# The front of the two expert stages, reordered: router ahead of the turns, inner scores behind the matrix of places, second exponential behind the gather

## The reference

```python
def hier_moe(h, router_g, router_g_b, router_e, router_e_b, w_gate, w_up, w_down):
    ...
    g_logits = (xt @ router_g + router_g_b).astype(f32)
    g_prob = jax.nn.softmax(g_logits, axis=-1)
    _, g_top = lax.top_k(g_logits, 1)
    p_group = jnp.take_along_axis(g_prob, g_top, axis=-1)
    e_logits = (jnp.einsum('td,gde->tge', xt, router_e) + router_e_b).astype(f32)
    e_sel = jnp.take_along_axis(e_logits, g_top[:, :, None], axis=1)[:, 0]
    top_v, top_i = lax.top_k(e_sel, TOP_K_INNER)
    top_w = jax.nn.softmax(top_v, axis=-1) * p_group
    inner = jnp.sum(jax.nn.one_hot(top_i, EXPERTS_PER_GROUP, dtype=f32) * top_w[..., None], axis=1)
    gates = jax.nn.one_hot(g_top[:, 0], N_EXPERT_GROUPS, dtype=f32)[:, :, None] * inner[:, None, :]
    out = jnp.zeros((xt.shape[0], d), f32)
    for gi in range(N_EXPERT_GROUPS):
        hid = jax.nn.silu(jnp.einsum('td,edf->tef', xt, w_gate[gi])) * jnp.einsum('td,edf->tef', xt, w_up[gi])
        hid = hid * gates[:, gi, :, None].astype(hid.dtype)
        out = out + jnp.einsum('tef,efd->td', hid, w_down[gi]).astype(f32)
    return out.reshape(bsz, s, d).astype(h.dtype)
```

## Time and profile before

| what | us |
|---|---|
| time, median of 3 runs (lowest to highest) | 3173.31 (3170.94 to 3181.55) |
| the profiled execution's own time | 3173.19 |
| its span in the trace | 3171.4 |
| busy: PE, DVE, ACT, POOL | 2880.9, 2026.5, 1645.3, 134.6 |
| chain that ended last, share of the span: PE, DVE, ACT, issue, DMA | 79%, 14%, 3%, 2%, 2% |

### The profile page before, as it was taken

The page is one execution under the profiler, slowest core; times in us unless marked ns, Lnnn a source line. Parts: engine busy times, 40 slices in busy tenths (PEclk is TensorE's granted clock), DMA queues, the critical chain, the costliest instruction groups (busy, mean ns, idle before and its releaser), DMA issues.

```text
span 3171.4 us, 54600 instructions
## 1 busy us (share of the span) xinstructions
PE 2880.9 (91%) x22896; PEld 2598.8 (82%) x22896; DVE 2026.5 (64%) x2543; ACT 1645.3 (52%) x2326; POOL 134.6 (4%) x164
## 2 busy tenths in 40 slices
PE   3778888689999999979999899999899979999999
PEld 3767666678877999867778788999799969998899
DVE  6866665579998555569999645444544684446444
ACT  1333342268887344448888535444544734445444
POOL 0013221000000020200000000000000000000000
PEclk7879999699999999979999989999899989999999
DMA  8630000259998537329999521554255404544253
GB/s 353 248 124 3 3 2 2 103 210 360 354 354 313 202 144 269 117 100 354 356 352 355 194 80 67 186 182 164 80 181 178 158 27 147 185 160 146 104 178 130
DMA packets 78119, 572.86 MB, mean 181 GB/s; under 512 B 8658, under 2 KB 8658, under 8 KB 9042
## 3 DMA queue, kind: packets, MB, share of 16 engines
q1 hardware_dynamic: 76752, 558.93, 47.3%
q10 hardware_dynamic: 1154, 10.90, 0.9%
HBM read 568.74 MB, written 1.05 MB: 180 GB/s over the span
## 4 chain that ended last, share of the span: by engine, by line
PE 79%; DVE 14%; ACT 3%; issue 2%; DMA 2%; DVEq 0%; POOL 0%; ACTq 0%; PEldq 0%
PE ps L1247 13%; PE ps L1174 12%; PE ps L811 9%; PE ps L812 9%; PE ps L813 9%; PE ps L1268 6%; DVE arena L2000 5%; DVE arena L1994 2%; DVE wl L1994 2%; DVE hl L1994 2%; DMA ring<-in_stream 1%; PE ps L832 1%; PE ps L831 1%; PE ps L830 1%; PE ps L853 1%
## 5 line engine op out<-in xcount | busy, mean ns | idle before, releaser
L1994 DVE TENSOR_TENSOR wl<-ring,wh 128x1024 fp32r<-128x1024 f32 (+1 forms) x560 | 937.8, 1695 | 636.1 <-ACT wh L1458 630.2
L1458 ACT ACTIVATE wh<-ring 128x1024 fp32r<-128x1024 f32 (+1 forms) x560 | 788.8, 1431 | 488.1 <-PE ps L813 323.0
L811 PE MATMUL ps<-hh,wh 128*128 128x256 f32 x2528 | 738.7, 292 | 79.5 <-DVE hl L1994 72.7
L812 PE MATMUL ps<-hh,wl 128*128 128x256 f32 x2528 | 725.8, 287 | 0.0
L813 PE MATMUL ps<-hl,wh 128*128 128x256 f32 x2528 | 725.2, 287 | 0.0
L811 PEld LDWEIGHTS ps<-hh,wh 128*128 128x128 f32 x2528 | 495.8, 196 | 94.3 <-issue 65.1
L812 PEld LDWEIGHTS ps<-hh,wl 128*128 128x128 f32 x2528 | 496.4, 196 | 3.2 <-issue 2.9
L813 PEld LDWEIGHTS ps<-hl,wh 128*128 128x128 f32 x2528 | 496.0, 196 | 0.0
L1174 PE MATMUL ps<-hidh,wh 128*128 128x256 f32 x1024 | 289.8, 283 | 0.0
L1174 PE MATMUL ps<-hidh,wl 128*128 128x256 f32 x1024 | 289.8, 283 | 0.0
L1174 PE MATMUL ps<-hidl,wh 128*128 128x256 f32 x1024 | 289.8, 283 | 0.0
(11 more groups left out here) (243 smaller groups left out, 4566.3 us busy)
## 6 DMA issues: line engine op xcount, KB each, us to landing
ring<-in_stream SPq DMA_DIRECT2D x532, 1024.0 KB, 5.0
arena<-in_wcmp ACTq DMA_DIRECT2D x2, 2048.0 KB, 11.2
arena<-in_lora ACTq DMA_DIRECT2D x1, 2048.0 KB, 10.9
arena<-in_atm ACTq DMA_DIRECT2D x1, 1762.0 KB, 8.3
x<-in_xT ACTq DMA_DIRECT2D x1, 1024.0 KB
out<-x SPq DMA_DIRECT2D x1, 1024.0 KB, 3.9
arena<-in_rwm ACTq DMA_DIRECT2D x1, 736.0 KB, 14.8
cols<-in_cols ACTq DMA_DIRECT2D x1, 719.0 KB
```

What stands on the lines that cost most here:

```text
L811: mm(out, w[0], h[0], start=first, stop=False)
L812: mm(out, w[1], h[0], start=False, stop=False)
L1458: return nc.scalar.activation(out, in_, ACT.Copy)
L1994: return v.tensor_tensor(out, a, b, op)
```

## The change

It changes the order of instructions in the front of both expert stages, and their banks and waits accordingly; the arithmetic is the same but for the order in which router products are summed.

- Router: one product writes the bias for both halves (72 columns), then the products of each pair of chunks follow as soon as the pair is there. The turns come behind the router, in the hi banks instead of the lo banks.
- VectorE: `norm` no longer does `flipped_low`; pair 0's low part comes behind the choice of the group, those of pairs 1 to 3 behind the eight blocks of the matrix of places. `m_P` counts after these eight blocks; the fifth part's two blocks have a count of their own, `m_P5`. `prep(q0 + 1)` moves from the start of the stage to behind the gather's low parts, and so do the inner scores.
- TensorE: the gather waits for the low part of each pair of chunks instead of all; `cleared` comes ahead of the wait for the gather's banks; `m_P5` is waited for ahead of the gather of the fifth part.
- ScalarE: the second exponential moves from behind the first casts of expert 1 to behind the gather's casts.

```diff
--- before.py
+++ after.py
@@ -333,8 +333,8 @@
 
 def _plan_moe(i):
     _plan(f"norm_cm{i}", 1)
-    _plan(f"xt{i}", 4)
     _plan(f"route{i}", 1)
+    _plan(f"xt{i}", 0, 4)
     _plan(f"rank{i}", 1)
     _plan(f"gather{i}", 8)
     _plan(f"moe{i}", 0, 4)
@@ -1196,20 +1196,23 @@
 
             def experts(i):
                 name, y0 = f"moe{i}", (AUX + 10) * i
+                t = claim("lo", LO[f"route{i}"])
+                route = [t[:, tt * 36:tt * 36 + 36] for tt in range(2)]
+                mm(t[:, 0:72].rearrange("p (t n) -> p t n", t=2), ones[0:1, :], rows[0:1, None, 36 * i:36 * i + 36].to_broadcast([1, 2, 36]),
+                   start=True, stop=False, skip_group_check=True)
                 for pr in range(4):
                     pe.wait_ge(src_ready, 4 * VER[name] + pr + 1)
-                    t = claim("lo", LO[f"xt{i}"] + pr)
+                    for k in (2 * pr, 2 * pr + 1):
+                        for tt in range(2):
+                            last = mm(route[tt], hf[:, k, tt * P:(tt + 1) * P], col(f"router{i}", 36 * k, 36), start=False, stop=k == C - 1,
+                                      skip_group_check=True)
+                last.then_inc(tile_ready["lo"], 1)
+                for pr in range(4):
+                    t = claim("hi", HI[f"xt{i}"] + pr)
                     for tt in range(2):
                         for k in range(2):
                             last = nc.tensor.transpose(t[:, (2 * tt + k) * P:(2 * tt + k + 1) * P], hf[:, 2 * pr + k, tt * P:(tt + 1) * P], ident)
-                    last.then_inc(tile_ready["lo"], 1)
-                t = claim("lo", LO[f"route{i}"])
-                for tt in range(2):
-                    o = t[:, tt * 36:tt * 36 + 36]
-                    for k in range(C):
-                        mm(o, hf[:, k, tt * P:(tt + 1) * P], col(f"router{i}", 36 * k, 36), start=k == 0, stop=False)
-                    last = mm(o, ones[0:1, :], rows[0:1, 36 * i:36 * i + 36], start=False, stop=True)
-                last.then_inc(tile_ready["lo"], 1)
+                    last.then_inc(tile_ready["hi"], 1)
                 pe.wait_ge(ev("m_og"), i + 1)
                 t = claim("lo", LO[f"rank{i}"])
                 og, earlier = MO[:, 384:392].rearrange("p (t n) -> p t n", t=2), amask("earlier")
@@ -1224,14 +1227,14 @@
                         last = mm(o, XKt[h][:, tt, k * P:(k + 1) * P], Pm[:, tt, a], start=j == 0, stop=j == 3)
                     return last
 
-                wait_h(name)
                 pe.wait_ge(ev("m_P"), i + 1)
                 for k in range(C):
+                    wait_part(name, k)
                     t = claim("lo", LO[f"gather{i}"] + k)
                     gather(t, k, slice(0, 512)).then_inc(tile_ready["lo"], 1)
+                cleared(name)
                 for m in range(LO[f"gather{i}"] + 4, LO[f"gather{i}"] + 8):
                     pe.wait_ge(free("lo", m), m // 4 + 1)
-                cleared(name)
 
                 def up(e, part):
                     b, g = b_up(e) + part, e // INNER
@@ -1282,6 +1285,7 @@
 
                 up(0, 0)
                 up(0, 1)
+                pe.wait_ge(ev("m_P5"), i + 1)
                 for a in range(2):
                     t = claim("y", y0 + a)
                     for k in range(4):
@@ -1631,9 +1635,9 @@
                 name, y0, q0 = f"moe{i}", (AUX + 10) * i, Q0[f"moe{i}"]
                 wait_done(act, LAST_READ[VERSIONS[VER[name] - 1]])
                 for pr in range(4):
-                    m = LO[f"xt{i}"] + pr
-                    ready(act, "lo", m)
-                    copy(XKt[0][:, :, pr * S:(pr + 1) * S], tile("lo", m).rearrange("p (t n) -> p t n", t=2)).then_inc(hh_ready, 1)
+                    m = HI[f"xt{i}"] + pr
+                    ready(act, "hi", m)
+                    copy(XKt[0][:, :, pr * S:(pr + 1) * S], tile("hi", m).rearrange("p (t n) -> p t n", t=2)).then_inc(hh_ready, 1)
                 prep(q0 + 1)
                 act.wait_ge(ev("group_arg"), i + 1)
                 fn(MO[:, 0:8], MO[:, 0:8], ACT.Exp).then_inc(ev("group_exp"), 1)
@@ -1641,6 +1645,8 @@
                     m = LO[f"gather{i}"] + k
                     ready(act, "lo", m)
                     copy(XTh[:, k, 0:512], tile("lo", m)).then_inc(ev("m_xh"), 1)
+                act.wait_ge(ev("pair_arg"), i + 1)
+                fn(MO[:, 8:10], MO[:, 8:10], ACT.Exp).then_inc(ev("pair_exp"), 1)
 
                 def high(e, part, x_):
                     b = b_down(e) if part == 2 else b_up(e) + part
@@ -1668,8 +1674,6 @@
                     copy(XTh[:, 4 * a:4 * a + 4, 512:640], tile("y", y0 + a).rearrange("p (k n) -> p k n", k=4)).then_inc(ev("m_xh"), 1)
                 high(1, 0, 0)
                 high(1, 0, 1)
-                act.wait_ge(ev("pair_arg"), i + 1)
-                fn(MO[:, 8:10], MO[:, 8:10], ACT.Exp).then_inc(ev("pair_exp"), 1)
                 swish(0)
                 high(1, 1, 0)
                 for a in range(3):
@@ -2291,16 +2295,15 @@
 
             def flipped_low(i, pr):
 
-                m = LO[f"xt{i}"] + pr
+                m = HI[f"xt{i}"] + pr
                 dve.wait_ge(hh_ready, 4 * VER[f"moe{i}"] + pr + 1)
                 a = slice(pr * S, (pr + 1) * S)
-                K(tt(XKt[1][:, :, a], tile("lo", m).rearrange("p (t n) -> p t n", t=2), XKt[0][:, :, a].bitcast(F32), SUB))
-                dve.sem_inc(free("lo", m), 1)
+                K(tt(XKt[1][:, :, a], tile("hi", m).rearrange("p (t n) -> p t n", t=2), XKt[0][:, :, a].bitcast(F32), SUB))
+                dve.sem_inc(free("hi", m), 1)
                 dve.sem_inc(h_ready, 1)
 
             def experts(i):
                 name, y0, q0 = f"moe{i}", (AUX + 10) * i, Q0[f"moe{i}"]
-                prep(q0 + 1)
                 m = LO[f"route{i}"]
                 ready(dve, "lo", m)
                 K(v.tensor_copy(Lr, tile("lo", m)[:, 0:72].rearrange("p (t n) -> p t n", t=2)))
@@ -2339,11 +2342,7 @@
                 tt(e4, gl, wide(mg, 4), SUB).then_inc(ev("group_arg"), 1)
                 og = first_of(gl, mg, 4, MO[:, 384:392].rearrange("p (t n) -> p t n", t=2))
                 dve.sem_inc(ev("m_og"), 1)
-                es, t8 = tmp(2, 8), tmp(2, 8)
-                for g in range(4):
-                    K(tt(t8 if g else es, Lr[:, :, 4 + 8 * g:12 + 8 * g], og[:, :, g:g + 1].to_broadcast([P, 2, 8]), MUL))
-                    if g:
-                        K(tt(es, es, t8, ADD))
+                flipped_low(i, 0)
                 m = LO[f"rank{i}"]
                 ready(dve, "lo", m)
                 t, rk, ro, cnt, big = tile("lo", m), tmp(2), tmp(2), tmp(2, 4), tmp(4)
@@ -2357,9 +2356,24 @@
                 dve.wait_ge(ev("m_pick"), i + 1)
                 for tt_ in range(2):
                     for g in range(GROUPS):
-                        ts(Pm[:, tt_, g * P:(g + 1) * P], amask("iota"), rk[:, tt_:tt_ + 1], og[:, tt_, g:g + 1], ALU.is_equal, MUL)
+                        last = ts(Pm[:, tt_, g * P:(g + 1) * P], amask("iota"), rk[:, tt_:tt_ + 1], og[:, tt_, g:g + 1], ALU.is_equal, MUL)
+                        if tt_ == 1 and g == GROUPS - 1:
+                            last.then_inc(ev("m_P"), 1)
+                for pr in range(1, 4):
+                    flipped_low(i, pr)
+                for tt_ in range(2):
                     last = ts(Pm[:, tt_, 512:640], amask("iota"), ro[:, tt_:tt_ + 1], None, ALU.is_equal)
-                last.then_inc(ev("m_P"), 1)
+                last.then_inc(ev("m_P5"), 1)
+                for k in range(C):
+                    m = LO[f"gather{i}"] + k
+                    dve.wait_ge(ev("m_xh"), (C + 2) * i + k + 1)
+                    tt(XTl[:, k, 0:512], tile("lo", m), XTh[:, k, 0:512].bitcast(F32), SUB).then_inc(free("lo", m), 1)
+                prep(q0 + 1)
+                es, t8 = tmp(2, 8), tmp(2, 8)
+                for g in range(4):
+                    K(tt(t8 if g else es, Lr[:, :, 4 + 8 * g:12 + 8 * g], og[:, :, g:g + 1].to_broadcast([P, 2, 8]), MUL))
+                    if g:
+                        K(tt(es, es, t8, ADD))
                 m1, m2 = tmp(2), tmp(2)
                 K(v.reduce_max(m1, es, AX_X))
                 o1 = first_of(es, m1, 8)
@@ -2367,10 +2381,6 @@
                 K(stt(e2, o1, NEG, es, MUL, ADD))
                 K(v.reduce_max(m2, e2, AX_X))
                 tt(MO[:, 8:10], m2, m1, SUB).then_inc(ev("pair_arg"), 1)
-                for k in range(C):
-                    m = LO[f"gather{i}"] + k
-                    dve.wait_ge(ev("m_xh"), (C + 2) * i + k + 1)
-                    tt(XTl[:, k, 0:512], tile("lo", m), XTh[:, k, 0:512].bitcast(F32), SUB).then_inc(free("lo", m), 1)
                 o2 = first_of(e2, m2, 8)
                 dve.wait_ge(ev("group_exp"), i + 1)
                 K(v.tensor_reduce(sg, e4, AX_X, ADD))
@@ -2752,7 +2762,7 @@
```

(2 more changed lines are left out.)

## The result

The changed kernel took 3141.96 us, the median of four runs (3134.92 to 3146.87), against 3174.82 us for the kernel before (four runs, 3170.94 to 3181.55). The ratio is 0.989, with a 95% interval from 0.9872 to 0.9908: 32.9 us less. The profiled execution took 3134.92 us, its span is 3133.1 us.

The account below looks back on a forecast made before the run. TensorE, 91% busy, bounds the kernel; gains lie in each expert stage's serial front. Cutting 69.05 and 66.66 us to 52.0 each saves 31.7, taking 3173.3 to 3141.6 us, range 3134 to 3149.

Parts of the forecast that it names:

- Norm to router: Front of each stage: first router product 1.58 us after VectorE's norm start, logits at 8.40 instead of 17.4.
- Ranks to matrix: Rank products 2.29 us, then VectorE and eight blocks: matrix of places ready 17.60 us after norm start, previously 24.9.
- the clock rises early: Rival: TensorE's busy front raises its clock; transposes, ranks and gather shorten, some 4.5 us less per layer, 3133; chance 0.07.
- Gather: Gather behind the matrix of places: 9.8 us, mean of both layers, lower bound 7.7; gathered parts at 27.4.
- Drain and up: After the gather: drain 1.49 us, up products from 28.9 taking 5.79, fifth part's gather 3.54, ending at 38.2.
- Gates: 20 gate records after the fifth part's gather: TensorE's 5.1 us wait gone by 0.3 margin, records 3.0, ending 41.2.
- the rival of a late VectorE: Rival: VectorE late at the gates, TensorE waits 1 to 3 us per layer, 3143.5 to 3147.5; chance 0.08.
- The clock falls in the gates: Rival: 20 gate records take 4.42 us at the low clock, slow transposes behind shaded by VectorE; 3144.4, chance 0.20.
- Gates to first down: VectorE's cast chain between gates and first down product stays 10.8 us, ending 52.0 after norm start.
- Loads: Sixth weight block's load issues about 31 us after norm start, hidden by over 10 us.
- Sum: Both stages: 17.05 us saved in layer 0 and 14.66 in layer 1, together 31.7, giving 3141.6.
- the rival worth 2.4 us a layer: Rival: router records well under 0.18 us follow the norm's pace, logits about 6.0 instead of 8.4; 3136.8, chance 0.01.

Follow-up runs that it names:

- fillers: Changed kernel plus products on constants: five ahead of the router, one behind each of its first three pairs, six ahead of the gather; 3135.38 us.
- the last: Against the combined one: inner scores back behind the gather, first hidden tile's copy and subtraction ahead of expert 2's casts; 3129.37 us, ratio 0.9853 to the kernel before.
- the combined one: Changed kernel plus fillers, early scores and down casts, second weight block's casts in halves, last place transposes later; 3130.67 us, ratio 0.9862 to the kernel before.
- the same six: Changed kernel plus only six products on constants in the gather's bank, while TensorE waits for the matrix of places; 3138.62 us.

## Why the prediction was right

3141.6 was predicted and 3141.96 measured. The chain and its links came as forecast; that the number fits within 0.4 us is luck. The stages gave 1.9 us more than the sum said, the median of the kernel before, from which the sum is taken, rose from 3173.31 to 3174.82 with its fourth run, and the changed kernel's own runs spread over 12 us. Inside the stage two terms were off in opposite directions, the ranks (1.2 us too long) and the gather (0.5 too short), and made up for each other in part. By its own steps, from the start of the norm, layer 0 / layer 1:

- *Norm to router.* Predicted 1.58 for the first product and 8.40 for the logits; 1.59, and 8.63 / 8.47. The order of router and transposes is worth 4.7 to 5.4 by the experiment.
- *Transposes.* Done at 12.04 predicted, 11.87 / 11.93.
- *Ranks to matrix.* 17.60 predicted, 16.15 / 16.32. The term of 2.29 for the ranks was mis-sized: they took 1.02 / 1.13 because the clock rose just ahead of them. The rival "the clock rises early" came true for this one term. (Its price of 4.5 us a layer was under its own terms, 1.8 + 1.1 + 2.1 = 5.1; with fillers 5.3 and 5.6 came.)
- *Gather.* 9.8 predicted, 10.25 / 10.42, because the clock had fallen again. The forecast had it right that the gather starts low.
- *Drain and up.* Start of the up products 28.9 predicted, 28.00 / 28.45; they took 5.81 against 5.79, and nothing stopped in their middle. The fifth part's gather ends at 37.34 / 37.78 (38.2).
- *Gates.* No wait, as predicted, and by the margin predicted: the fifth part's first tile freed the bank at 36.91 (37.9 predicted) and TensorE came at 37.34 (38.2), 0.4 us later where 0.3 was forecast. VectorE's gate values were ready at 35.45 (36.6); behind them VectorE still idled 0.78 us for ScalarE's copy of that tile, so the rival of a late VectorE needed a delay of 1.2 us and not of 0.3. Gates 2.72 / 2.64 (3.0).
- *The clock falls in the gates.* It did, but behind them more than in them: they took 2.7, not 4.42, at a granted clock of 0.77 in layer 0 and 0.80 in layer 1, and the transposes and the first up products at 1.2 GHz lay in the shade of VectorE's chain, as that rival said of them.
- *Gates to first down.* 10.79 in both layers, 10.8 predicted: VectorE's casts in the order that the prediction names.
- *Loads.* The issue 30 us after the norm's start, no wait in the loop; the run with the early low part shows that its place costs nothing.
- *Sum.* 33.65 us from the two stages, 31.7 predicted; the medians differ by 32.9. Undoing two parts of the change, the exponential's place and the order of transposes and router, costs 6.7 + 4.7 in layer 0 and 7.6 + 5.4 in layer 1, of 18.20 and 15.45. Undoing the places of the scores and of the second block's low part costs nothing. The rest, 6.8 and 2.4 us, was not undone by itself: low parts out of the norm, eight blocks instead of ten ahead of the gather, the zero products under the drain, and in layer 0 up products of 5.81 instead of 7.22. It is read from the chains of waits alone.

The prediction set the Trainium skill (TensorE: Matmul & The Clock Gate, Back-to-back issue gap) against the trace: a narrow product should take N columns over the clock, with a floor near 25 ns. That is the section's figure for a product by itself; it also says that in a stream of weight loads and products both set the spacing. The trace does not agree with the first figure, and the rows decided rightly. The router took 0.22 us a record at 1.2 GHz, and with fillers 0.93 / 8 = 0.116 at 2.4 GHz. TensorE's weight loads were busy in all of the router's 7.00 us too (34 of them, first row of the clock above), so no run here tells whether the loads or the products set that pace. Only in the runs with fillers ahead of it did the router follow the norm's pace, which was the rival worth 2.4 us a layer that I gave 0.01; by the rows it failed at the low clock alone.

What stays open: why the clock rose ahead of the ranks in some stages and only in the gather in others, of the same kernel. In the changed kernel's two profiles ranks and gather together take 11.2 to 11.6 us either way. That is no rule: in layer 1 of the kernel with the late exponential, whose order is the same up to there, ranks of 1.95 were followed by a gather of 10.46, 12.4 together.

## What to carry to other kernels

A stretch in which every engine waits for the next is costed link by link from one mark to the next; measure by the same marks afterwards, since a stage of 50 us repeats within 0.7 us while the times of the whole program spread over 12. A wait on TensorE can cost its length and then the low clock behind it: here 5.1 us of waiting were worth 6.7, and constant products in time that is idle anyway brought 5 us a layer, as long as they do not run into the wait's end at the low clock. When a chain gets shorter, read again what stands in the queue ahead of the operation that the other engine waits for: the hidden tile's subtraction stood behind the next block's casts in every kernel up to the last, and TensorE waited for it in the kernel before (2.15 us), in the changed one (0.66) and in the combined one (1.13).

## What was not expected of the hardware

The clock's level in the same code differs between executions: 0.70 and 1.00 in 15 us of the RWKV stage, which both kernels share, and 1.02 or 1.95 us for the rank products in the two layers of one execution of the changed kernel. In that execution the layer that saw the clock rise early and fall again was no shorter than the one that saw it rise late (11.3 and 11.2 us for ranks and gather). And fillers are not safe by themselves: the same six cost nothing and made the stage 2.2 us shorter in layer 0, and in layer 1 they took 5.33 us and won nothing.
